# The modulation vector of a conditioned decoder: sixteen of its twenty-four pieces with the weights as the stationary operand

## The chip, the cores and the metric

The kernel runs on one core of a Trainium2 chip. The time is the device time of one execution in microseconds (us), the median over several runs. Engines are named as in the profile: PE (TensorE, matmuls; PEld are its loads of the stationary operand), DVE (VectorE), ACT (ScalarE), POOL (GpSimd), SP (SyncE, which here only issues transfers).

## The reference

One decoder layer works on 2048 prompt positions and 8 x 8 sample positions of width 1024. Shift, scale and gate of its two halves come from a conditioning vector: one row for the prompt, eight for the samples.

```python
def decoder_layer(x, c, ...):
    mod = jnp.einsum("bd,de->be", jax.nn.silu(c), w_ada) + b_ada      # w_ada: 1024 x 6144
    sh1, sc1, g1, sh2, sc2, g2 = jnp.split(mod[:, None, :], 6, axis=-1)
    h = x * (1.0 + sc1) + sh1
    mix, ... = mixer_block(h, ...)          # input projection, three token mixers, output projection
    x = layer_norm(DEEPNORM_ALPHA * x + g1 * mix, ln1_g, ln1_b)
    h2 = x * (1.0 + sc2) + sh2
    f = jnp.einsum("btf,fd->btd", jnp.square(jax.nn.relu(jnp.einsum("btd,df->btf", h2, w_up))), w_down)
    x = layer_norm(DEEPNORM_ALPHA * x + g2 * f, ln2_g, ln2_b)
```

## The kernel before

The prompt is worked in four groups of 512 positions, the samples ride with the last. First comes the mixer of each group: four slabs of w_in give the rows v (`v_slab`), twelve more (`fm_product`, F0 to F11) the other columns of the projection by features, DVE turns them into the mixer's three parts, and eight slabs of w_out close it. Then the MLP of all groups follows. Products are taken in three passes of a high and a low part (`mm3`); ACT and POOL make these parts from the raw slab, which SP fetches.

The modulation vector `mod` (9 rows x 6144) is computed in 24 pieces of 256 columns, `ada_product(u)` on PE. Each needs 1 MB of w_ada and the bias columns on 9 partitions. The 9 columns of silu(c), turned to features (`siluT`), are the stationary operand, the weights stream. The sums come out as 9 rows in PSUM; DVE adds the bias rows (`ada_add`, L1479), SP stores the rows to `mod_rows` in DRAM, from where the gates are later fetched. Shift and scale are needed by features, so PE turns every piece back with two transposes (`ada_turn`, L1110), and DVE copies the result into `modT` (`ada_turned`, L1488 and L1490; one is added to the scale). The semaphore `ada_T` counts these copies, and product u waits for the copy of piece u-2, whose bank it takes.

Pieces 0 to 7 are shift and scale of the first half, computed while the first group's x is turned (`x0_transposes`, L1159) and the first v slabs are worked. Pieces 8 to 23 stand in the stages of the first group's mixer, in an order written out by hand (`mixer_stages`): two after each of F0 to F3, one after each of F4 to F11. There `ada_turn(u-1)` follows `ada_product(u)` on PE, and `ada_add(u)`, `ada_turned(u-1)` stand behind the evacuation of the slab product on DVE. The stage "B" makes a bias table (DVE L1628), the stages "S" are the position mixing (DVE L1609). After piece 23 comes `second_modulation`, and then the next group's x is turned (`x_transposes`, L1219).

Of the kernel before, what the change touches and what calls it, by code (L numbers as in the profile page):

```python
# [233 lines left out]
def mixer_stages(s, vector):  # L234


    nt, first = tiles_of(s), s == 0
    F = [("F", n) for n in range(N_FM)]
    S01, S23 = ("S", [0, 1], 0 if nt == 4 else 1), ("S", [2, 3], 2 if nt == 4 else 3)
    if nt == 5:  # L240
        S4 = ("S", [4], 0)
        a = [S4, ("V", 1), F[0], ("V", 1)] if vector else [F[0], S4]
        a += [F[1], S01, ("V", 2), F[2], S23, F[3], F[4]]
    elif vector or first:
        a = [F[0], F[1], S01, ("V", 2), F[2], S23, F[3], F[4]]
    else:
        a = F[0:4] + [S01, F[4], S23]
    a += [F[5], F[6], F[7], ("M", 0), F[8], F[9], ("M", 1), F[10], F[11]]
    if first:
        out, u = [], ADA_FIRST  # L250
        for x in a:
            out.append(x)
            if x[0] == "F":
                for _ in range(2 if x[1] < 4 else 1):
                    out.append(("A", u))
                    u += 1
                if x[1] == 0:
                    out.append(("B", 0))
        a = out + [("E", u - 1)]
    return [x for x in a if vector or x[0] != "V"]  # L260


def decoder_layer_kernel(nc, x_prompt, x_sample, c_prompt, c_sample, state_conv, state_pool,
# [5 lines left out]
    with ctx:  # L269
# [66 lines left out]
        st = sb("st", [P, 5, 2, 6])  # L336
        siluT = sb("siluT", [P, KD * (1 + NB)])
        ln_now = (sb("mv", [P, 5, 2]), sb("rstd", [P, 5]), sb("rtmp", [P, 5]))
        ln_end = (sb("mv_end", [P, 5, 2]), sb("rstd_end", [P, 5]), sb("rtmp_end", [P, 5]))
# [43 lines left out]
        ada_mm = sem("ada_mm")  # L383
        ada_row = sem("ada_row")
        ada_tr = sem("ada_tr")
        ada_T = sem("ada_T")
        ada_out = [sem(f"ada_out{i}") for i in range(4)]
        x0_tr = sem("x0_tr")
# [108 lines left out]

        def ada_bias(u):
            return gs[0:1 + NB, ADA_COLS * (u % 4):ADA_COLS * (u % 4) + ADA_COLS]

# [16 lines left out]
        def _(sp):  # L517
# [5 lines left out]

            def ada_bias_in(u):
                if u >= 4:
                    sp.wait_ge(ada_tr, u - 3)
                    sp.wait_ge(ada_out[u % 4], 16 * (u // 4))
                sp.dma_start(ada_bias(u), bcast(b_ada[0, ada_col(u):ada_col(u) + ADA_COLS], 1 + NB)
                             ).then_inc(ada_in[u % 4], 16)

            def ada_rows_out(u):
                sp.wait_ge(ada_row, u + 1)
                sp.dma_start(mod_rows[:, ada_col(u):ada_col(u) + ADA_COLS], ada_bias(u)
                             ).then_inc(ada_out[u % 4], 16)
# [31 lines left out]
            for u in range(1, 3):  # L566
                ada_weights(u)
                ada_bias_in(u)
            x0_load(0)
# [54 lines left out]
            def weight_mix(g):  # L624
# [8 lines left out]
                for c, (after, buf) in enumerate(MIX_JOBS):  # L633
                    turn = [x for _, x in MIX_JOBS[0:c]].count(buf)
                    b, q, cols = mix_view(c)
                    if g == after:
                        if turn:
                            sp.wait_ge(mix_stored[buf], 16 * turn)
                        elif buf == 0:
                            sp.wait_ge(xs_tr, 1)  # L640
                        else:
                            sp.wait_ge(ada_tr, N_ADA)
                        for i in range(2):
# [45 lines left out]
            ada_weights(3)  # L689
            ada_bias_in(3)  # L690
            for n in range(2):
                slab(n, free=False)
            ada_rows_out(0)
            ada_piece(4)
# [21 lines left out]
            slab(21)  # L716
            for i in range(4):
                sp.wait_ge(ada_out[i], 16 * (N_ADA // 4))
            sp.dma_start(g1row[:, :], bcast(mod_rows[0, G1 * D:G1 * D + D], P)).then_inc(g1_loaded, 16)
# [368 lines left out]
        def _(pe):  # L1088
# [5 lines left out]
            def ada_product(u):  # L1094
                pe.wait_ge(ada_in[u % 4], 32 * (u // 4 + 1))
                if u >= 2:
# [3 lines left out]
                buf = ada_buffer(u)  # L1100
                for k in range(KD):
                    ins = pe.matmul(ps[0:1 + NB, 1 + 2 * (u % 2), 0:ADA_COLS],
                                    siluT[:, (1 + NB) * k:(1 + NB) * (k + 1)], buf[:, k, :],
                                    start=(k == 0), stop=(k == KD - 1))
                ins.then_inc(ada_mm, 1)

            def ada_turn(u):
                pe.wait_ge(ada_row, u + 1)
                for q in range(2):
                    ins = pe.transpose(ps[:, 1 + 2 * (u % 2), (1 + NB) * q:(1 + NB) * (q + 1)],  # L1110
                                       ada_bias(u)[:, P * q:P * q + P], ident[0:1 + NB, 0:1 + NB])
                ins.then_inc(ada_tr, 1)

            pe.wait_ge(s_c, 32)
            pe.wait_ge(s_ident, 1)
            for k in range(KD):
                ins = pe.transpose(ps[:, 0, (1 + NB) * k:(1 + NB) * (k + 1)],
                                   c_rows[0:1 + NB, P * k:P * k + P], ident[0:1 + NB, 0:1 + NB])
            ins.then_inc(s_cT, 1)
            pe.wait_ge(s_silu, 1)  # L1120
# [34 lines left out]
            def x0_transposes(k):  # L1155
                if k >= 2:
                    pe.wait_ge(x_tmp, k - 1)
                for t in range(4):
# [4 lines left out]
            def ada_next(u):  # L1163
                ada_product(u)
                ada_turn(u - 1)

            ada_next(1)
            for n in range(3):
                ada_next(2 * n + 2)
# [4 lines left out]
                ada_next(2 * n + 3)  # L1174
                if n < 2:
                    v_slab(0, n)
            ada_turn(ADA_FIRST - 1)
            x0_transposes(6)
# [44 lines left out]
            def mixer(s):  # L1223
# [5 lines left out]
                for stage in mixer_stages(s, False):  # L1229
# [35 lines left out]
                    elif stage[0] == "A":  # L1265
                        ada_product(stage[1])
                        if stage[1] > ADA_FIRST:
                            ada_turn(stage[1] - 1)
                    elif stage[0] == "E":
                        ada_turn(stage[1])  # L1270
                    else:
# [187 lines left out]
        def _(dve):  # L1459
# [22 lines left out]
            def ada_turned(u):  # L1482
                dve.wait_ge(ada_tr, u + 1)
# [3 lines left out]
                if q // KD == SC1:  # L1487
                    dve.tensor_scalar(dst, src, 1.0, None, ALU.add).then_inc(ada_T, 1)  # L1488
                else:
                    dve.tensor_copy(dst, src).then_inc(ada_T, 1)  # L1490

            def second_modulation():
                dve.wait_ge(ada_T, N_ADA)
                sh2, sc2 = (modT[:, q * KD:q * KD + KD, :] for q in (SH2, SC2))
                lng, lnb = (lnT[:, i, :].unsqueeze(2).to_broadcast([P, KD, 1 + NB]) for i in range(2))
                do(dve.tensor_scalar(sc2, sc2, 1.0, None, ALU.add))
                do(dve.tensor_tensor(scale2[:, :, :], sc2, lng, ALU.mult))
# [271 lines left out]
            def mixer(s):  # L1769
# [28 lines left out]
                for stage in mixer_stages(s, True):  # L1798
# [16 lines left out]
                    elif stage[0] == "A":  # L1815
                        ada_add(stage[1])
                        if stage[1] > ADA_FIRST:
                            ada_turned(stage[1] - 1)
                    elif stage[0] == "E":
                        ada_turned(stage[1])  # L1820
                        second_modulation()
# [26 lines left out]

            def ada_next(u):
                ada_add(u)  # L1850
                ada_turned(u - 1)

            ada_next(1)
            for n in range(3):
                ada_next(2 * n + 2)
                x0_feature(2 * n)
                x0_feature(2 * n + 1)
                ada_next(2 * n + 3)
            ada_turned(ADA_FIRST - 1)
            x0_feature(6)  # L1860
# [241 lines left out]
```

## Time and profile before

| | |
|---|---|
| median of 3 runs | 2225.09 us (2224.11 to 2225.3) |
| profiled execution | 2226.75 us, of it span 2225.0 us |
| PE busy | 2117.9 us, 95% |
| DVE busy | 1494.7 us, 67% |
| mean granted PE clock | 0.977 |

The profile is of one execution. Busy times of PE contain the latency of each pass, so that passes overlap in it: the distance between starts is the cost of one. A count of passes is twice that of plain fp32 matmuls, since each is run in two.

### The profile page before, as it was taken

To read this page: it belongs to the slowest core of one execution; us is meant where nothing else is said; L and a number is where in the kernel's file an instruction comes from. 1 tells how busy PE (TensorE), PEld (TensorE's weight loads), DVE (VectorE), ACT (ScalarE), POOL (GpSimd) and SP (SyncE) were. 2 spreads that over 40 slices of the span, in tenths; PEclk is the share of its full clock that TensorE was granted. 3 is DMA by queue.
4 is the path that set the end of the run, shared out by engine and by line. 5 is a ranking of instruction groups with operands and counts; after the bars stand their busy time and mean duration, and the time that the engine had idled before them with its cause. 6 is when DMAs were issued, how large, how long until landed. Compare 5 with 4: busy or idle time off the path is not lost.

```text
span 2225.0 us, 27801 instructions
## 1 busy us (share of the span) xinstructions
PE 2117.9 (95%) x10342; PEld 1750.2 (79%) x10342; DVE 1494.7 (67%) x2055; ACT 861.6 (39%) x1173; POOL 1448.8 (65%) x1109
## 2 busy tenths in 40 slices
PE   7989999999989999999989999989999999999995
PEld 4556787887889788888868888868888888999983
DVE  1554479678587665567778757687757777665677
ACT  1201322323212354445544545634454544444440
POOL 3323578685424367787777778867878866666664
PEclk9999999999999999999989999999999999999997
DMA  8546588695333254454624564534564533454331
GB/s 262 157 154 228 194 240 252 202 280 167 91 124 114 88 185 145 159 182 138 194 86 144 179 217 148 173 104 142 180 218 142 170 119 114 147 170 143 114 124 43
DMA packets 324089, 357.78 MB, mean 161 GB/s; under 512 B 16280, under 2 KB 256105, under 8 KB 323954
## 3 DMA queue, kind: packets, MB, share of 16 engines
q1 hardware_dynamic: 323954, 355.99, 50.7%
q8 instruction: 83, 1.36, 0.3%
q14 instruction: 52, 0.43, 0.1%
HBM read 321.34 MB, written 34.59 MB: 160 GB/s over the span
## 4 chain that ended last, share of the span: by engine, by line
PE 63%; DVE 11%; POOL 2%; issue 1%; ACT 1%; DVEq 0%; ACTq 0%
PE ps L1090 21%; PE ps L1092 20%; PE ps L1091 20%; PE ps L1354 1%; POOL acc L883 1%; DVE xt L1915 1%; DVE hid_a L1873 1%; POOL w_hilo L856 1%; DVE mix L1534 0%; DVE htmp L1716 0%; DVE pair_sums L1891 0%; PE ps L1423 0%; DVE acc L1977 0%; DVE pair_sums L1892 0%; DVE acc L1609 0%
## 5 line engine op out<-in xcount | busy, mean ns | idle before, releaser
L856 POOL TENSOR_TENSOR w_hilo<-w_raw,w_hilo 128x512 fp32r<-128x512 f32 x890 | 1270.1, 1456 | 719.5 <-ACT w_hilo L935 719.1
L935 ACT ACTIVATE w_hilo<-w_raw 128x1024 fp32r<-128x1024 f32 x445 | 469.9, 1058 | 720.3 <-PE ps L1092 610.3
L1090 PE MATMUL ps<-hA,w_hilo 128*128 128x512 f32 (+1 forms) x1760 | 621.9, 353 | 8.2 <-ACT htmp L993 3.2
L1091 PE MATMUL ps<-hA,w_hilo 128*128 128x512 f32 (+1 forms) x1760 | 620.3, 352 | 0.0
L1092 PE MATMUL ps<-hA,w_hilo 128*128 128x512 f32 (+1 forms) x1760 | 620.2, 352 | 0.0
L1090 PEld LDWEIGHTS ps<-hA,w_hilo 128*128 128x128 f32 x1760 | 332.2, 189 | 51.4 <-issue 7.5
L1091 PEld LDWEIGHTS ps<-hA,w_hilo 128*128 128x128 f32 x1760 | 332.3, 189 | 41.8
L1092 PEld LDWEIGHTS ps<-hA,w_hilo 128*128 128x128 f32 x1760 | 332.0, 189 | 41.5
L1965 DVE TENSOR_TENSOR acc<-acc,ps 128x512 f32<-128x512 f32 x270 | 178.4, 686 | 78.1 <-PE ps L1092 75.1
L1090 PE MATMUL ps<-w_hilo,hid_a 128*128 128x512 f32 x450 | 179.9, 400 | 25.8 <-DVE acc L1962 20.5
L1090 PE MATMUL ps<-w_hilo,hid_b 128*128 128x512 f32 x450 | 176.5, 392 | 1.6 <-POOL w_hilo L856 1.6
L1091 PE MATMUL ps<-w_hilo,hid_a 128*128 128x512 f32 x450 | 177.0, 393 | 0.0
L1092 PE MATMUL ps<-w_hilo,hid_a 128*128 128x512 f32 x450 | 176.8, 393 | 0.0
L1092 PE MATMUL ps<-w_hilo,hid_b 128*128 128x512 f32 x450 | 176.2, 392 | 0.0
L1091 PE MATMUL ps<-w_hilo,hid_b 128*128 128x512 f32 x450 | 176.1, 391 | 0.0
L986 ACT ACTIVATE htmp<-ps 128x512 f32<-128x512 f32 x96 | 57.2, 596 | 280.1 <-PE ps L1092 274.4
L1891 DVE TENSOR_TENSOR pair_sums<-htmp 128x256 f32<-128x256 f32 x62 | 33.2, 536 | 190.1 <-ACT htmp L996 189.8
L1090 PEld LDWEIGHTS ps<-w_hilo,hid_a 128*128 128x128 f32 x450 | 85.4, 190 | 44.4 <-issue 24.2
L1090 PE MATMUL ps<-w_hilo,mix 128*128 128x512 f32 (+1 forms) x272 | 109.4, 402 | 7.5 <-DVE mix L1534 7.5
L1091 PE MATMUL ps<-w_hilo,mix 128*128 128x512 f32 (+1 forms) x272 | 107.9, 397 | 0.0
L1092 PE MATMUL ps<-w_hilo,mix 128*128 128x512 f32 (+1 forms) x272 | 107.8, 396 | 0.0
L1090 PEld LDWEIGHTS ps<-w_hilo,hid_b 128*128 128x128 f32 x450 | 85.1, 189 | 20.3 <-POOL w_hilo L856 2.3
(233 smaller groups left out, 3000.2 us busy)
## 6 DMA issues: line engine op xcount, KB each, us to landing
w_raw<-in_w_up SPq DMA_DIRECT2D x128, 512.0 KB, 4.0
w_raw<-w_mix SPq DMA_DIRECT2D x124, 512.0 KB, 3.2
w_raw<-in_w_down SPq DMA_DIRECT2D x97, 512.0 KB, 3.6
w_raw<-in_w_in SPq DMA_DIRECT2D x64, 512.0 KB, 4.8
xt<-in_w_ada SPq DMA_DIRECT2D x22, 1024.0 KB
w_raw<-in_w_out SPq DMA_DIRECT2D x32, 512.0 KB, 4.8
xt<-x_norm SPq DMA_DIRECT2D x19, 512.0 KB, 5.7
xt<-in_w_down SPq DMA_DIRECT2D x36, 256.0 KB, 5.2
```

The source lines that it names most:

```text
L856: ins = pool.tensor_tensor(W[:, g % SLOTS, 1, cols], raw[:, g % RAW, cols], W[:, g % SLOTS, 0, cols], ALU.subtract)
L883: ins = pool.tensor_tensor(a, a, rows[:, G2_ROW, cols], ALU.mult)
L935: act.activation(W[:, g % SLOTS, 0, :], raw[:, g % RAW, :], ACT.Copy).then_inc(hi_done, 1)
L986: act.activation(x[:, 0:GT], ps[:, f % 2, :], ACT.Relu).then_inc(up_read, 1)
L1090: pe.matmul(out, w_hi, x_hi, start=start, stop=False)
L1091: pe.matmul(out, w_hi, x_lo, start=False, stop=False)
L1092: return pe.matmul(out, w_lo, x_hi, start=False, stop=stop)
L1354: pe.matmul(ps[:, 2 + h, :], x, W[:, w, part, HALF * p:HALF * p + HALF], start=start and part == 0, stop=False)
L1873: signal(dve.tensor_tensor(flat_part(h, 1, a, k), x, flat_part(h, 0, a, k), ALU.subtract), hid_ready, n)
L1891: do(dve.tensor_tensor(s1, a21, a22, ALU.add))
L1915: do(dve.scalar_tensor_tensor(x, x, ALPHA, acc[0:r, t, :], ALU.mult, ALU.add))
L1965: dve.tensor_tensor(a, a, src, ALU.add).then_inc(d_evac, 1)
```

## The change

The order of the columns over the pieces changes for u of 8 and more: even pieces are now gates (first G1, then G2), odd ones shift and scale of the second half. Gates keep the old way up to the rows, and have no transposes. The other sixteen pieces take each 128 x 128 block of weights as the stationary operand and stream the 9 columns of `siluT`: 16 matmuls of 9 columns, whose sums are already by features. Their bias is loaded once, as 48 rows of 128, turned by PE, and kept in `biasT` with one added at the scales; DVE adds it on the way to `modT`. Bias loads and row stores remain for the gates only.

```diff
-    return ADA_COLS * u
+    n = (u - ADA_FIRST) // 2
+    return ((G1, G2) if is_gate(u) else (SH2, SC2))[n // 4] * D + ADA_COLS * (n % 4)
+def is_gate(u):
+    return u >= ADA_FIRST and u % 2 == 0
...
             def ada_rows_out(u):
-                sp.wait_ge(ada_row, u + 1)
+                if is_gate(u):
+                    sp.wait_ge(ada_T, u + 1)
...
+            sp.dma_start(gs[0:6 * KD, 0:P], b_ada[0].rearrange("(q p) -> q p", p=P)).then_inc(s_c, 16)
             ada_weights(0)
-            ada_bias_in(0)
...
             for u in range(1, 3):
                 ada_weights(u)
-                ada_bias_in(u)
...
             def ada_product(u):
-                pe.wait_ge(ada_in[u % 4], 32 * (u // 4 + 1))
+                pe.wait_ge(ada_in[u % 4], 16 * (u // 4 + 1))
...
-                for k in range(KD):
-                    ins = pe.matmul(ps[0:1 + NB, 1 + 2 * (u % 2), 0:ADA_COLS],
-                                    siluT[:, (1 + NB) * k:(1 + NB) * (k + 1)], buf[:, k, :],
-                                    start=(k == 0), stop=(k == KD - 1))
+                bank = 1 + 2 * (u % 2)
+                if is_gate(u):
+                    for k in range(KD):
+                        ins = pe.matmul(ps[0:1 + NB, bank, 0:ADA_COLS], siluT[:, (1 + NB) * k:(1 + NB) * (k + 1)],
+                                        buf[:, k, :], start=(k == 0), stop=(k == KD - 1))
+                else:
+                    for q in range(2):
+                        for k in range(KD):
+                            ins = pe.matmul(ps[:, bank, (1 + NB) * q:(1 + NB) * (q + 1)], buf[:, k, P * q:P * q + P],
+                                            siluT[:, (1 + NB) * k:(1 + NB) * (k + 1)],
+                                            start=(k == 0), stop=(k == KD - 1))
                 ins.then_inc(ada_mm, 1)
...
-            def ada_turn(u):
-                pe.wait_ge(ada_row, u + 1)
-                for q in range(2):
-                    ins = pe.transpose(ps[:, 1 + 2 * (u % 2), (1 + NB) * q:(1 + NB) * (q + 1)],
-                                       ada_bias(u)[:, P * q:P * q + P], ident[0:1 + NB, 0:1 + NB])
-                ins.then_inc(ada_tr, 1)
...
-            def ada_add(u):
+            def ada_turned(u):
                 dve.wait_ge(ada_mm, u + 1)
-                dve.tensor_tensor(ada_bias(u), ps[0:1 + NB, 1 + 2 * (u % 2), 0:ADA_COLS], ada_bias(u),
-                                  ALU.add).then_inc(ada_row, 1)
...
+                if is_gate(u):
+                    dve.wait_ge(ada_rows_in[u // 2 % 2], 16 * (gate_turn(u) // 2 + 1))
+                    rows_ = ada_rows(u)
+                    dve.tensor_tensor(rows_, ps[0:1 + NB, 1 + 2 * (u % 2), 0:ADA_COLS], rows_,
+                                      ALU.add).then_inc(ada_T, 1)
+                    return
...
-                    dve.tensor_copy(dst, src).then_inc(ada_T, 1)
+                dve.tensor_tensor(dst, src, biasT[:, q:q + 2].unsqueeze(2).to_broadcast([P, 2, 1 + NB]),
+                                  ALU.add).then_inc(ada_T, 1)
...
                     elif stage[0] == "A":
-                        ada_add(stage[1])
-                        if stage[1] > ADA_FIRST:
-                            ada_turned(stage[1] - 1)
+                        ada_turned(stage[1])
```

PE around pieces 14 and 15, which follow F3 (the pool part). Before, from the end of F3 to the start of F4:

```order
L1092 MATMUL ps<-hA,w_hilo 128x512
L1102 MATMUL ps<-xt,siluT 9x256 [waits ada_T,ada_in2]
L1102 MATMUL ps<-xt,siluT 9x256 x7
L1110 MATMUL ps<-ident,gs 128x9 [waits ada_row]
L1110 MATMUL ps<-ident,gs 128x9
L1102 MATMUL ps<-xt,siluT 9x256 [waits ada_T,ada_in3]
L1102 MATMUL ps<-xt,siluT 9x256 x7
L1110 MATMUL ps<-ident,gs 128x9 [waits ada_row]
L1110 MATMUL ps<-ident,gs 128x9
L1090 MATMUL ps<-hA,w_hilo 128x512 [waits lo_done,fm_evac]
```

After, the same place (L1100 to L1102 are now the three passes of `mm3`, L1114 a gate piece, L1120 a feature piece):

```order
L1102 MATMUL ps<-hA,w_hilo 128x512
L1114 MATMUL ps<-xt,siluT 9x256 [waits ada_T,ada_in2]
L1114 MATMUL ps<-xt,siluT 9x256 x7
L1120 MATMUL ps<-siluT,xt 128x9 [waits ada_T,ada_in3]
L1120 MATMUL ps<-siluT,xt 128x9 x15
L1100 MATMUL ps<-hA,w_hilo 128x512 [waits lo_done,fm_evac]
```

Both pairs of transposes have gone; piece 15 has 16 matmuls in place of 8.

DVE at the same place. Before, from the end of the pool part's work (F3) to that of the u part (F4):

```order
L1534 TENSOR_TENSOR spl<-htmp,spl 128x512 [waits s_chain]
L1479 TENSOR_TENSOR gs<-ps,gs 9x256 [waits ada_mm,d_ready]
L1490 COPY modT<-ps 128x18 [waits ada_tr]
L1479 TENSOR_TENSOR gs<-ps,gs 9x256 [waits ada_mm]
L1490 COPY modT<-ps 128x18 [waits ada_tr]
L1745 TENSOR_TENSOR acc<-ps,acc 128x512 [waits slab_used]
```

After:

```order
L1546 TENSOR_TENSOR spl<-htmp,spl 128x512 [waits s_chain]
L1496 TENSOR_TENSOR gs<-ps,gs 9x256 [waits ada_rows_in1,ada_mm,d_ready]
L1502 TENSOR_TENSOR modT<-ps,biasT 128x18 [waits ada_mm]
L1757 TENSOR_TENSOR acc<-ps,acc 128x512 [waits slab_used]
```

The first L1490 before belongs to piece 13, the second to piece 14; L1496 after belongs to piece 14 and L1502 to piece 15. Piece 13's copy, on which PE's product 15 waits, now stands ahead of this place, behind F2.

## Rows read from the trace of the kernel before

**Rows 1.** The page, its first part: busy time, share of span, instructions.

```profile
PE 2117.9 (95%) x10342; PEld 1750.2 (79%) x10342; DVE 1494.7 (67%) x2055; ACT 861.6 (39%) x1173; POOL 1448.8 (65%) x1109
```

**Rows 2.** Stretches: length, busy by engine (PE, PEld, DVE, ACT, POOL), clock, DMA.

```profile
0.00:32.00 32.00, 17.76 (x80) 8.73 (x80) 4.25 (x10) 3.07 (x4) 6.04 (x45) 0.94 0.86 250
32.00:84.80 52.80, 52.28 (x244) 33.71 (x244) 20.41 (x48) 12.36 (x14) 29.98 (x24) 0.97 0.70 220
84.80:236.00 151.20, 137.23 (x621) 84.47 (x621) 75.75 (x150) 15.35 (x16) 46.08 (x36) 0.95 0.51 166
236.00:2225.00 1989.00, 1910.68 (x9400) 1623.33 (x9398) 1394.33 (x1850) 830.83 (x1139) 1366.67 (x1004) 0.98 0.50 157
```

**Rows 3.** Groups by form, 0 to 236 us: busy, mean ns, idle before.

```profile
L1102 PE MATMUL ps<-xt,siluT 128*9 128x256 f32 x352 | 85.9, 401 | 15.8 <-DVE modT L1490 9.7 <-DMA gs<-in_b_ada 6.1
...
L1479 DVE TENSOR_TENSOR gs<-ps,gs 9x256 f32<-9x256 f32 x24 | 9.9, 412 | 70.2 <-PE ps L1102 70.1
...
L1110 PE MATMUL ps<-ident,gs 9*128 9x9 f32 x48 | 6.9, 213 | 0.7 <-DVE gs L1479 0.7
```

**Rows 4.** PE's timeline, 14 to 236 us: start, duration, instructions, idle before.

```profile
14.63 1.04 PE L1130 MATMUL ps<-ident,g1row 128*128 128x128 f32 x8
17.26 3.62 PE L1102 MATMUL ps<-xt,siluT 128*9 128x256 f32 x16 [1.59 <-DMA gs<-in_b_ada]
...
37.47 0.50 PE L1090 MATMUL ps<-w_hilo,hA 128*128 128x512 f32 x1
...
43.13 3.62 PE L1102 MATMUL ps<-xt,siluT 128*9 128x256 f32 x16
46.69 0.29 PE L1110 MATMUL ps<-ident,gs 9*128 9x9 f32 x2
46.90 0.33 PE L1159 MATMUL ps<-ident,acc 128*128 128x128 f32 x1
...
109.22 5.30 PE L1102 MATMUL ps<-xt,siluT 128*9 128x256 f32 x16 [2.05 <-DVE modT L1490]
...
152.12 4.90 PE L1102 MATMUL ps<-xt,siluT 128*9 128x256 f32 x16 [6.47 <-DVE modT L1490]
...
235.81 1.06 PE L1219 MATMUL ps<-ident,xs 128*128 128x128 f32 x8 [0.36 <-DVE modT L1490]
```

**Rows 5.** PE's waits in the whole span: total us, times, longest.

```profile
PE ps L1102 <- DVE modT L1490: 9.7, 4, 6.5
...
PE ps L1110 <- DVE gs L1479: 0.7, 2, 0.4
```

**Rows 6.** DVE's timeline, 142 to 152 us.

```profile
142.02 0.17 DVE L1695 COPY acc<-pcarry 128x15 f32<-128x15 f32 x1 [1.63 <-PE ps L1092]
...
151.82 0.15 DVE L1490 COPY modT<-ps 128x18 f32<-128x18 f32 x1
```

**Rows 7.** PEld's timeline: loads of transposes, then full-width loads for 128 columns.

```profile
46.68 0.20 PEld L1110 LDWEIGHTS ps<-ident,gs 9*128 9x128 f32 x2 [0.43 <-issue]
...
617.89 0.18 PEld L1090 LDWEIGHTS ps<-wsS,spl 64*128 64x128 f32 x1 [0.16 <-issue]
...
619.12 0.19 PEld L1092 LDWEIGHTS ps<-wsS,spl 64*128 64x128 f32 x1
```

**Rows 8.** Stretches of 2 us; columns as in rows 2.

```profile
92.00:94.00 2.00, 1.01 (x8) 0.79 (x7) 1.26 (x4) 0.00 (x0) 0.21 (x1) 1.00 0.99 304
94.00:96.00 2.00, 0.94 (x6) 0.77 (x6) 0.84 (x2) 0.00 (x0) 0.00 (x0) 1.00 1.04 331
96.00:98.00 2.00, 1.94 (x6) 1.56 (x7) 1.39 (x3) 0.00 (x0) 0.00 (x0) 0.69 0.90 306
98.00:100.00 2.00, 2.00 (x7) 1.51 (x6) 0.00 (x0) 0.00 (x0) 0.00 (x0) 0.50 0.06 21
```

**Rows 9.** SP's timeline: the dearest small bias load, and the eight copies.

```profile
12.54 1.69 SPq L528 DMA_DIRECT2D gs<-in_b_ada  x1
...
17.63 6.00 SPq L578 DMA_DIRECT2D acc<-acc  x8
```

More of the change, by code:

```diff
@@ L259, in mixer_stages @@
         a = out + [("E", u - 1)]
-    return [x for x in a if vector or x[0] != "V"]
+    return [x for x in a if vector or x[0] not in ("V", "E")]
 def decoder_layer_kernel(nc, x_prompt, x_sample, c_prompt, c_sample, state_conv, state_pool,
@@ L383, in decoder_layer_kernel @@
         ada_mm = sem("ada_mm")
-        ada_row = sem("ada_row")
-        ada_tr = sem("ada_tr")
         ada_T = sem("ada_T")
-        ada_out = [sem(f"ada_out{i}") for i in range(4)]
+        ada_rows_in = [sem(f"ada_rows_in{i}") for i in range(2)]
+        ada_out = [sem(f"ada_out{i}") for i in range(2)]
+        s_biasT = sem("s_biasT")
         x0_tr = sem("x0_tr")
@@ L496, in ada_buffer, with ada_rows @@
             return t.rearrange("p t (a n) -> p (t a) n", a=4)
-        def ada_bias(u):
-            return gs[0:1 + NB, ADA_COLS * (u % 4):ADA_COLS * (u % 4) + ADA_COLS]
+        def ada_rows(u):
+            return gs[0:1 + NB, ADA_COLS * (2 + u // 2 % 2):ADA_COLS * (2 + u // 2 % 2) + ADA_COLS]
         def hid(b, pair):
@@ L522, in ada_weights, with ada_rows_load @@
                              ).then_inc(ada_in[u % 4], 16)
[L524 to L529, printed above, removed]
+            def ada_rows_load(u):
+                if is_gate(u):
+                    if gate_turn(u) >= 2:
+                        sp.wait_ge(ada_out[u // 2 % 2], 16 * (gate_turn(u) // 2))
+                    sp.dma_start(ada_rows(u), bcast(b_ada[0, ada_col(u):ada_col(u) + ADA_COLS], 1 + NB)
+                                 ).then_inc(ada_rows_in[u // 2 % 2], 16)
             def ada_rows_out(u):
-                sp.wait_ge(ada_row, u + 1)
-                sp.dma_start(mod_rows[:, ada_col(u):ada_col(u) + ADA_COLS], ada_bias(u)
-                             ).then_inc(ada_out[u % 4], 16)
+                if is_gate(u):
+                    sp.wait_ge(ada_T, u + 1)
+                    sp.dma_start(mod_rows[:, ada_col(u):ada_col(u) + ADA_COLS], ada_rows(u)
+                                 ).then_inc(ada_out[u // 2 % 2], 16)
             def ada_piece(u):
@@ L538, in ada_piece @@
                 ada_rows_out(u - 3)
-                ada_bias_in(u)
+                ada_rows_load(u)
             def x0_load(t):
@@ L567, in _ @@
                 ada_weights(u)
-                ada_bias_in(u)
             x0_load(0)
@@ L716, in _ @@
             slab(21)
-            for i in range(4):
-                sp.wait_ge(ada_out[i], 16 * (N_ADA // 4))
+            for i in range(2):
+                sp.wait_ge(ada_out[i], 16 * (N_ADA - ADA_FIRST) // 4)
             sp.dma_start(g1row[:, :], bcast(mod_rows[0, G1 * D:G1 * D + D], P)).then_inc(g1_loaded, 16)
@@ L1157, in x0_transposes @@
                     pe.wait_ge(x_tmp, k - 1)
+                elif k == 0:
+                    pe.wait_ge(s_biasT, 1)
                 for t in range(4):
@@ L1161, in x0_transposes @@
                 ins.then_inc(x0_tr, 1)
[L1163 to L1167, printed above, removed]
+            ada_product(1)
             for n in range(3):
-                ada_next(2 * n + 2)
+                ada_product(2 * n + 2)
                 if n == 0:
@@ L1475, in signal, with bias_turned @@
                 dve.wait_ge(sem_, value)
-            def ada_add(u):
-                dve.wait_ge(ada_mm, u + 1)
-                dve.tensor_tensor(ada_bias(u), ps[0:1 + NB, 1 + 2 * (u % 2), 0:ADA_COLS], ada_bias(u),
-                                  ALU.add).then_inc(ada_row, 1)
-            def ada_turned(u):
-                dve.wait_ge(ada_tr, u + 1)
+            def bias_turned():
+                dve.wait_ge(s_cT, 1)
+                do(dve.tensor_copy(biasT[:, :], ps[:, 4, 0:6 * KD]))
+                do(dve.tensor_scalar(biasT[:, SC1 * KD:SC1 * KD + KD], biasT[:, SC1 * KD:SC1 * KD + KD], 1.0, None,
+                                     ALU.add))
+                signal(dve.tensor_scalar(biasT[:, SC2 * KD:SC2 * KD + KD], biasT[:, SC2 * KD:SC2 * KD + KD], 1.0,
+                                         None, ALU.add), s_biasT, 1)
+            def ada_turned(u):
+                dve.wait_ge(ada_mm, u + 1)
+                if is_gate(u):
+                    dve.wait_ge(ada_rows_in[u // 2 % 2], 16 * (gate_turn(u) // 2 + 1))
[3 more added lines that the diff above has]
+                    return
                 q = ada_col(u) // P
@@ L1840, in mixer @@
                     signal(normalise(x, x, t, ln_end), xn_dve, 2 * s + t - 1)
-            ada_add(0)
+            bias_turned()
             dve.wait_ge(s_prepe, 1)
@@ L1847, in _ @@
             dve.tensor_copy(prep[:, 1, :].rearrange("p (b n) -> p b n", b=2), ps[:, 6:8, :]).then_inc(s_pret, 1)
[L1849 to L1853, printed above, removed]
+            ada_turned(0)
+            ada_turned(1)
             for n in range(3):
-                ada_next(2 * n + 2)
+                ada_turned(2 * n + 2)
                 x0_feature(2 * n)
                 x0_feature(2 * n + 1)
-                ada_next(2 * n + 3)
-            ada_turned(ADA_FIRST - 1)
+                ada_turned(2 * n + 3)
             x0_feature(6)
```

27 lines of the change are left out of this document (9 added, 18 removed).

## The prediction

> **What bounds the kernel now.** I read the table by stretches first, then the groups by line, PE's waits, and PE's and DVE's timelines inside the modulation part. PE is busy 95% of the span, the next engine 67% [rows 1]. The change touches only the first 236 us. In its first 32 us PE is busy for 17.8 us and the DMA engines for 0.86 of the time: transfers decide there. From 32 to 84.8 us PE is full (52.3 of 52.8), and from 84.8 to 236 it has 137 of 151 us [rows 2]. So from 32 us on, every PE nanosecond of the modulation pieces is on the path, and so is every PE wait; before that almost nothing of them is. After 236 us nothing is edited and PE stays full (1911 of 1989 us), so a gain or loss at 236 us is carried to the end.
>
> A piece now is 16 passes of a 256-column moving weight against 9 stationary columns (8 matmuls in fp32, two passes each), then two small transposes [rows 3]. A piece at the full clock takes 3.56 us to the start of the transposes, and the transposes 0.21 us to the next instruction: 43.13, 46.69, 46.90 [rows 4]. PE waits in this part are mostly one kind: the piece waits for DVE's copy of transposes, 9.7 us in four waits; two more, 0.7 us together, end at a transpose [rows 5]. The longest is 6.47 us, before 152.12. DVE's rows say why: the copy that releases it (151.82) stands behind the whole pooling step that began at 142.02 [rows 6]. After two of these waits, of 2.05 and 6.47 us, the piece takes 5.30 and 4.90 us in place of 3.62 [rows 4]: passes at about twice the distance at their start, as at 1.2 GHz in place of 2.4, after an idle engine. Elsewhere the table of clocks shows that level, 0.50 for 98 to 100 us [rows 8].
>
> **The change part by part.** Of 24 pieces, 8 (gates) keep their matmuls; 16 become 32 passes with 128 stationary and 9 moving columns.
>
> Removed transposes: 24 pairs. Two lie in the part that transfers decide, 22 behind it. 22 x 0.21 = 4.6 us gained.
>
> The new passes. No row shows a full-width fp32 weight with 9 moving columns. The nearest are the loads of 128 columns that are no transposes, 0.18 to 0.19 us each from start to end [rows 7]. What counts is the distance from one load to the next. Where 12 such full-width loads follow each other with short moving operands, the first starts at 617.89 and the last at 619.12: 1.23/11 = 0.112 us [rows 7]. 32 x 0.112 = 3.58 us a piece, against 3.56 now. With 0.1 us for the first load, which nothing covers, I take +0.1 us x 13 (the feature pieces from u = 3 on) = 1.3 us lost. Bounds: if the loads went like those of the small transposes, two in 0.20 us where a full-width transposing load lasts about 0.14, they would be some 0.064 us apart [rows 7], a piece 2.05 us, and the kernel gains 13 x 1.5 = 20 us more. If load and pass did not overlap at all, 0.188 each, a piece is 6.0 us and 13 x 2.5 = 32 us are lost. I take 0.112, since its row has the same kind of load (no transpose) and the same width. The Trainium skill (TensorE: Matmul & The Clock Gate, LDWEIGHTS) puts the load at its column count over 1.2 GHz whatever the rows, 107 ns for 128; by that alone a piece would be 3.4 us. It says too (Weight-path perf modes) that fp32 gets no faster weight load. The rule speaks against this change: moving 9 columns in place of 256 buys nothing, because the load takes the place of the stream, and the row above agrees.
>
> The waits. Now piece u waits for the copy of piece u-2, and DVE makes that copy in its turn of piece u-1, behind the evacuation of the slab product before it. After the change DVE empties piece u-2 in that piece's own turn, one turn earlier, which the order's rows show: no row of u-1 stands ahead of it. So in stages with two pieces the second no longer waits for the evacuation work between. All 9.7 us go, and the 0.7 us of the two at a transpose [rows 5]. What is late next at the long one: piece 14 (3.6), piece 15 (3.6) and slab product F4 (5.66, as 37.47 to 43.13) give PE 12.8 us after F3, while DVE is through with pooling and the two small copies 151.97 - 142.02 = 10 us after it begins, right behind F3 [rows 4, 6]. The next piece needs DVE only then: 3 us of room. In the second pooling step the room is wider. The transfers do not bite: a piece's 1 MB is issued when piece u-2 has ended, some 9 us or more before its use, and the DMA engines are half idle from 84.8 us on [rows 2].
>
> The clock after the waits: 5.30 + 4.90 - 2 x 3.62 = 3.0 us gained, since the idle time that went before is gone.
>
> At the end of the part PE still waits for DVE's last piece, about the 0.36 us it waits now; nothing gained.
>
> Off the path: DVE loses 24 additions of 0.41 us [rows 3], 16 of them replaced by copies that now add the bias, about 0.16 us as today's copies. It gains four small ones at the start, about 0.8 us, while PE waits for weights. SP loses 32 small DMAs of rows and biases. Three of them stand at the start, the dearest with 1.69 us of issue, and one comes in their place; but the x tiles that end the start are issued behind the 8 copies at 17.63, which wait for DVE's copy of the turned w_s and not for SP, so I put this at nothing [rows 9]. If SP did decide, it would be at most some 2 us of gain.
>
> Sum: 4.6 + 9.7 + 0.7 + 3.0 - 1.3 = 16.7 us. I take 16. The profiled execution has 2226.75 us (span 2225.0 and 1.75 around), 1.7 above the median of the runs; it would come to 2210.7, and the median of the runs, 2225.09, to 2209.
>
> **The rivals.**
> First: the clock. This is the one that ends on the other side. Between 92 and 96 us PE streams for half the time or less (busy 1.01 and 0.94 of 2 us, with latencies counted in), and the clock is down to 0.69 and 0.50 in the next two rows, 96 to 100 us [rows 8]. One such low stretch costs what the piece at 109.22 shows: 5.30 - 3.62 = 1.7 us [rows 4]. A pass of 256 columns takes 0.216 us ((3.62 - 0.38)/15, the last pass of a piece lasting 0.38), so 9 columns some 0.008 us of each 0.112. If the clock follows what streams through the array, a feature piece is emptier than that stretch was. If it follows whether PE has instructions in hand (loads or the drain of each pass included), a piece is full. Nothing before has loads without streaming, so the trace cannot tell. For the first view: 9-column stationary pieces hold the clock, so width does not matter, moving time may. For the second: even the 8 transposes at 14.63, followed by 1.6 us of waiting, left the piece at 17.26 at full clock, 3.62 us [rows 4]. The Trainium skill says of transposes that they do not count as busy (TensorE: Matmul & The Clock Gate, Part 4); this row speaks against it for these ones, and of weight loads the page says nothing. Price: 8 single pieces with one low stretch each, 8 x 1.7, and 5 in the stretch from 32 to 72 us where pieces stand close together and run at half speed themselves, 5 x 3.4: 30.6 us. Less the 16.7: +14, 2239 us. From half that price to 3.4 us for all 13 pieces, -1 to +27. It decides from about ten low stretches on.
>
> Second: the wait comes back elsewhere. If DVE is the bound of the slab stages, the 9.7 us and 3.0 us show up again as waits of slab products for evacuation. Then only 4 us are left: 2221. Against it: DVE is busy for half of the stretch from 84.8 to 236 us, 75.8 of 151.2 [rows 2].
>
> Third: loads do not overlap the passes (bound above): 16.7 - 32 = +15, 2240 us. The row with 0.112 speaks against it.
>
> Fourth: loads 0.064 us apart: 2209 - 20 = 2189.
>
> **How the numbers follow.** Forecast 0.46, clock 0.38, wait elsewhere 0.07, no overlap 0.04, cheap loads 0.05. The forecast's own range is 2203 to 2216 (load distance 0.105 to 0.12 is 13 x 32 x 0.007 = 3 us either way, waits 3 us). With the clock's case in, the range is 2203 to 2245; outside are the cheap loads and the worst of the clock, together under 0.2. What a measurement of this kernel can tell from no change is 0.2%, 4.5 us. Faster: 0.46, 0.05 and a part of the wait case and of the mild end of the clock: 0.56. Same 0.08, slower 0.36.
>
> **What would show it.** The groups of the pieces (now L1102) split into 8 gate pieces of 16 passes and 16 feature pieces of 32; the loads of the latter 188 ns long and 0.112 us apart; PE's wait on modT near 0.3 us in place of 9.7; the granted clock 1.00 from 36 to 236 us but for the stretch at 97 to 100; the first transposes of the next group of tiles at about 219 us in place of 235.81 [rows 4]. I am wrong if the windows behind feature pieces show 0.5 to 0.8 of the clock, if loads are 0.15 us or more apart, or if slab products wait for DVE where they did not.

## The result and the profile after

The changed kernel takes 2239.74 us (median of 4 runs, 2235.91 to 2240.24) beside 2225.2 us of the kernel before on the same chip: a ratio of 1.0053, 95% interval 1.0036 to 1.007. It is 14.5 us slower where 16 us of gain were forecast. The kernel before has medians of 2225.2 to 2230.5 us on the chips used below, so each run there is given as a ratio to it on the same chip too. The profiled execution has 2239.93 us and a span of 2238.2 us.

The stretches of the kernel after, with the bounds of [rows 2]; columns as there:

```profile
0.00:32.00 32.00, 25.32 (x121) 24.63 (x122) 2.81 (x9) 1.51 (x2) 6.04 (x45) 1.00 0.80 227
32.00:84.80 52.80, 51.89 (x249) 47.52 (x248) 9.84 (x21) 12.01 (x14) 20.17 (x17) 0.77 0.59 190
84.80:236.00 151.20, 148.72 (x736) 112.58 (x735) 79.93 (x149) 16.42 (x17) 52.88 (x42) 0.90 0.58 179
```

The column before the last two is the clock: 0.77 and 0.90 where [rows 2] have 0.97 and 0.95. PE looks busier than before (148.7 us against 137.2): its idle time went, and slow passes took its place. Even so the column says too little: up to the first fall that it shows, at 52 us here, it reads 1.00 whatever the passes do. Three passes of a slab product, each of 512 columns, start 1.28 us apart up to 46 us and 0.68 us apart behind it (next rows), so PE ran at half clock until about 46 us. Before, the first fall that it shows is at 28 us.

PE's timeline after: start, duration, instruction, idle before. L1114 is a gate piece, L1120 a feature piece, L1228 the turning of the next group's x:

```profile
17.63 7.00 PE L1120 MATMUL ps<-siluT,xt 128*128 128x9 f32 x32 [0.26 <-DMA xt<-in_w_ada]
24.48 6.98 PE L1120 MATMUL ps<-siluT,acc 128*128 128x9 f32 x32
...
34.16 7.00 PE L1120 MATMUL ps<-siluT,xt 128*128 128x9 f32 x32 [0.91 <-DMA xt<-in_w_ada]
41.01 0.77 PE L1100 MATMUL ps<-w_hilo,hA 128*128 128x512 f32 x1
42.44 0.63 PE L1100 MATMUL ps<-w_hilo,hA 128*128 128x512 f32 x1
43.72 0.63 PE L1100 MATMUL ps<-w_hilo,hA 128*128 128x512 f32 x1
...
47.51 0.39 PE L1100 MATMUL ps<-w_hilo,hA 128*128 128x512 f32 x1
48.19 0.39 PE L1100 MATMUL ps<-w_hilo,hA 128*128 128x512 f32 x1
...
48.87 3.63 PE L1120 MATMUL ps<-siluT,xt 128*128 128x9 f32 x32
52.36 0.31 PE L1173 MATMUL ps<-ident,acc 128*128 128x128 f32 x1
...
138.10 3.62 PE L1114 MATMUL ps<-xt,siluT 128*9 128x256 f32 x16
141.66 4.03 PE L1120 MATMUL ps<-siluT,xt 128*128 128x9 f32 x32
...
243.92 1.94 PE L1228 MATMUL ps<-ident,xs 128*128 128x128 f32 x8 [0.43 <-DVE modT L1502]
```

Three things stand here. A feature piece at full clock takes 3.63 us, passes (3.63 - 0.17)/31 = 0.112 us apart, the distance that [rows 7] gave (0.17 us is the length of the last pass). At half clock it takes 7.00 us, and the slab product behind it starts in the same state. And piece 15 at 141.66 follows its neighbour with no wait, where [rows 4] show 6.47 us before 152.12. The turning of x starts at 243.92 in place of 235.81, and its 8 transposes take 1.94 us in place of 1.06: the clock has fallen once more behind the last piece.

PE's waits after, whole span: none of a piece for DVE is left; [rows 5] had 9.7 us there.

```profile
PE ps L1120 <- DMA xt<-in_w_ada: 4.0, 3, 2.9
...
PE ps L1228 <- DVE modT L1502: 0.4, 1, 0.4
```

Stretches of 2 us after, around a pair of feature pieces (48.87 to 60.4, with the turning of eight tiles of x between them at 52.36):

```profile
50.00:52.00 2.00, 2.00 (x20) 2.00 (x20) 0.00 (x0) 0.00 (x0) 0.59 (x1) 1.00 0.03 8
52.00:54.00 2.00, 2.00 (x15) 2.00 (x15) 0.26 (x2) 0.81 (x2) 0.00 (x0) 0.70 0.06 18
54.00:56.00 2.00, 2.00 (x11) 2.00 (x11) 1.90 (x4) 1.69 (x2) 0.24 (x1) 0.50 0.95 333
...
64.00:66.00 2.00, 2.00 (x6) 1.61 (x5) 0.00 (x0) 0.00 (x0) 0.00 (x0) 0.50 0.00 0
66.00:68.00 2.00, 2.00 (x9) 1.58 (x9) 0.00 (x0) 0.00 (x0) 0.00 (x0) 0.89 0.00 0
```

PE is busy for the full 2 us in every row, and up to 56 us PEld too, and yet the clock falls to 0.50 and stays there into the slab product that begins at 60.4. No idle engine stands before this fall, unlike the ones of [rows 4].

**The balance.** What the clock takes can be read from such rows: (1 - clock) x length, with 0.5 for the time up to 46 us that the column misses. From 36 us to the turning of x it is 6.8 us before and 32.3 us after (27.3 by the column and 5.0). Piece 3 starts at 34.16 in place of 32.17, so the start costs 2.0 us. From there to the turning of x, before and after:

```profile
32.17:235.81 203.64, 189.31 (x862) 117.98 (x863) 95.87 (x195) 27.71 (x30) 76.06 (x60) 0.96 0.56 180
34.16:243.92 209.76, 206.85 (x1026) 166.00 (x1027) 90.99 (x174) 27.93 (x30) 75.71 (x60) 0.87 0.56 173
```

This stretch is 6.1 us longer. PE's idle time in it went from 14.3 to 2.9 us, 11.4 less, and 4.6 us of transposes went. Low clock in it is 33.2 us in place of 8.7, 24.5 more. Together that would be 8.5 us. Part of the rest is that a low stretch takes a little less than half of its length: passes of 512 columns are 0.427 us apart at half clock and 0.228 at full, 0.47 of it. That leaves some 0.9 us open. The turning of x moved by 2.0 + 6.1 = 8.1 us.

Behind the part the span grows by another 13.2 - 8.1 = 5.1 us. The code there is the same. The rows from there to 1080 us hold 17.1 us of low clock after and 11.9 before. Whether the change had a part in that is not shown: the run with 2 repeats below, as long in its first part, has 10.2 there.

### The profile page after: what moved, and what is told of

Its sections match the earlier page's. It is cut to its first block, busy times and chain, and to the rows that moved or that the text cites. A ratio compares the mean times of both kernels' runs of the same rounds, so it can differ in the third digit from the quotient of the medians.

```text
span 2238.2 us, 28147 instructions
## 1 busy us (share of the span) xinstructions
PE 2148.2 (96%) x10551; PEld 1818.4 (81%) x10551; DVE 1491.7 (67%) x2033; ACT 861.6 (38%) x1173; POOL 1449.6 (65%) x1109
## 4 chain that ended last, share of the span: by engine, by line
PE 63%; DVE 11%; POOL 2%; issue 1%; ACT 1%; DVEq 0%; ACTq 0%
PE ps L1100 20%; PE ps L1101 20%; PE ps L1102 20%; PE ps L1359 1%; POOL acc L893 1%; DVE xt L1920 1%; DVE hid_a L1878 1%; POOL w_hilo L866 1%; DVE htmp L1728 0%; DVE pair_sums L1896 0%; PE ps L1428 0%; DVE mix L1546 0%; DVE acc L1982 0%; DVE pair_sums L1897 0%; DVE acc L1621 0%
## 5 line engine op out<-in xcount | busy, mean ns | idle before, releaser
L1100 PE MATMUL ps<-hA,w_hilo 128*128 128x512 f32 (+1 forms) x1760 | 626.5, 356 | 8.1 <-ACT htmp L1003 3.2
L1102 PE MATMUL ps<-hA,w_hilo 128*128 128x512 f32 (+1 forms) x1760 | 623.8, 354 | 0.0
L1100 PEld LDWEIGHTS ps<-hA,w_hilo 128*128 128x128 f32 x1760 | 335.0, 190 | 54.1 <-issue 9.2
L1102 PEld LDWEIGHTS ps<-hA,w_hilo 128*128 128x128 f32 x1760 | 334.9, 190 | 42.5
L1100 PE MATMUL ps<-w_hilo,hid_a 128*128 128x512 f32 x450 | 179.7, 399 | 24.5 <-DVE acc L1967 20.5
L1100 PE MATMUL ps<-w_hilo,hid_b 128*128 128x512 f32 x450 | 176.6, 393 | 2.5 <-POOL w_hilo L866 2.5
L1102 PE MATMUL ps<-w_hilo,hid_a 128*128 128x512 f32 x450 | 176.6, 392 | 0.0
L1102 PE MATMUL ps<-w_hilo,hid_b 128*128 128x512 f32 x450 | 176.4, 392 | 0.0
L1100 PEld LDWEIGHTS ps<-w_hilo,hid_a 128*128 128x128 f32 x450 | 85.4, 190 | 43.2 <-issue 24.2
L1100 PE MATMUL ps<-w_hilo,mix 128*128 128x512 f32 (+1 forms) x272 | 109.4, 402 | 7.5 <-DVE mix L1546 7.5
L1102 PE MATMUL ps<-w_hilo,mix 128*128 128x512 f32 (+1 forms) x272 | 107.3, 394 | 0.0
L1100 PEld LDWEIGHTS ps<-w_hilo,hid_b 128*128 128x128 f32 x450 | 85.1, 189 | 21.0 <-POOL w_hilo L866 2.9
```

What stands on the lines that cost most here:

```text
L1100: pe.matmul(out, w_hi, x_hi, start=start, stop=False)
L1102: return pe.matmul(out, w_lo, x_hi, start=False, stop=stop)
```

## Experiments

Each run changes the changed kernel. The theories when the first four runs were chosen: A, the clock follows the time in which columns stream through the array, and weight loads do not count; B, the wide loads or the lack of transposes bring it down; C, the loss comes from the start or from the pieces' new order.

**14 repeats.** The same loads, but the 9 columns are streamed 14 times through a stride of zero; only the first nine sums are read.

```diff
-                            ins = pe.matmul(ps[:, bank, (1 + NB) * q:(1 + NB) * (q + 1)], buf[:, k, P * q:P * q + P],
-                                            siluT[:, (1 + NB) * k:(1 + NB) * (k + 1)],
-                                            start=(k == 0), stop=(k == KD - 1))
+                            r = repeats(u)
+                            out = ps[:, bank, PIECE * q:PIECE * q + (1 + NB) * r].rearrange("p (r n) -> p r n", r=r)
+                            x = siluT[:, (1 + NB) * k:(1 + NB) * (k + 1)].unsqueeze(1).to_broadcast([P, r, 1 + NB])
+                            ins = pe.matmul(out, buf[:, k, P * q:P * q + P], x, start=(k == 0), stop=(k == KD - 1))
```

(`repeats(u)` gives 14, PIECE is 128, and DVE reads its sums at 128 * q. The reading side is left out here.)

> The feature pieces stream each 9 columns of silu 14 times (126 columns in place of 9) against the same 32 weight loads; the extra sums are not read. Nothing else differs from the changed kernel. Theory A (the clock follows the time in which columns stream through the array): the granted clock stays at 1.00 from about 36 us to the end of the modulation part but for the stretch after the bias table, a pass still takes about 0.108 us because the load sets it, and the time falls to where the forecast had it without the clock's fall, 2208 to 2214 us. Theory B (the clock falls because of the wide loads themselves, or of the missing transposes, whatever streams): same clock as the changed kernel, 2240 us. Theory C (the loss is not the clock's but comes from the start or from the order of the pieces): 2235 to 2240 us.

Measured: 2209.48 us (2208.89 to 2210.38), ratio to the kernel before 0.9919 (0.9903 to 0.9934), within A's range. B and C fall: loads, order, and missing transposes are those of the changed kernel, and 30 us have gone. The pieces and the part's end:

```profile
7.39 5.55 PE L1130 MATMUL ps<-siluT,xt 128*128 128x126 f32 x32 [2.77 <-DMA xt<-in_w_ada]
17.41 3.84 PE L1130 MATMUL ps<-siluT,xt 128*128 128x126 f32 x32 [1.75 <-DMA xt<-in_w_ada]
...
212.30 3.73 PE L1130 MATMUL ps<-siluT,xt 128*128 128x126 f32 x32
216.46 1.07 PE L1236 MATMUL ps<-ident,xs 128*128 128x128 f32 x8 [0.43 <-DVE modT L1510]
```

A piece of 126-column passes lasts 3.73 us, (3.73 - 0.27)/31 = 0.112 us a pass: fourteen times the stream for no time. Already the second piece runs at full clock, though the clock falls once more in PE's wait for x (0.50 from 29 to 38 us).

**7, 4 and 2 repeats.** The same edit with r = 7, 4, 2.

> As the kernel with 14 repeats, with 7: 63 columns stream per load, some 0.05 us of each 0.108. Theory A: in between; the trace of before fell after a stretch that streamed for some 40% of its time, so at about half the clock may hold or fall now and then: 2210 to 2225 us. Theory B and C: 2240 us.

> As the kernel with 14 repeats, with 4: 36 columns stream per load, 0.03 us of each 0.108, less than the 40% after which the clock fell in the kernel before. Theory A: most feature pieces bring a fall again: 2226 to 2240 us. A theory by which only the almost empty passes of 9 columns count as idle (the drain of a pass counted in) would leave it near the kernel with 7 repeats, 2212 to 2218 us.

> With 2 repeats, 18 columns, 0.015 us of each 0.108. Theory A: as the changed kernel, 2234 to 2242 us.

Measured: 2215.5 (2212.32 to 2215.66; ratio 0.9942, 0.9925 to 0.9958), 2234.93 (2224.71 to 2241.16; ratio 1.0022, 1.0004 to 1.004) and 2239.48 us (2235.16 to 2241.26; ratio 1.0051, 1.0034 to 1.0068), each within the range that theory A gave it. The ten runs with 4 repeats scatter over 16 us. The table of stretches, from 36 to 84 and from 84 to 216 us, first with 14 repeats:

```profile
36.00:84.00 48.00, 48.00 (x297) 42.67 (x296) 18.43 (x41) 11.01 (x13) 29.75 (x24) 0.98 0.69 211
84.00:216.00 132.00, 128.48 (x715) 97.18 (x714) 72.02 (x129) 15.35 (x16) 45.54 (x36) 1.00 0.61 189
```

With 7 repeats, the same two stretches:

```profile
36.00:84.00 48.00, 48.00 (x290) 43.28 (x291) 15.12 (x27) 12.04 (x14) 27.89 (x22) 1.00 0.71 223
84.00:216.00 132.00, 128.47 (x693) 96.38 (x692) 74.19 (x141) 14.73 (x16) 45.77 (x36) 0.99 0.62 193
```

With 4 repeats:

```profile
36.00:84.00 48.00, 48.00 (x244) 43.71 (x245) 7.60 (x17) 9.40 (x11) 23.13 (x20) 0.82 0.59 183
84.00:216.00 132.00, 129.59 (x665) 98.82 (x663) 73.81 (x141) 15.36 (x16) 41.75 (x32) 0.92 0.60 186
```

With 2 repeats:

```profile
36.00:84.00 48.00, 48.00 (x233) 44.63 (x234) 6.78 (x17) 9.02 (x11) 18.93 (x16) 0.76 0.55 172
84.00:216.00 132.00, 129.59 (x650) 98.59 (x649) 72.15 (x140) 15.74 (x17) 44.64 (x34) 0.91 0.61 186
```

And the changed kernel, which streams the columns once:

```profile
36.00:84.00 48.00, 48.00 (x232) 44.21 (x232) 7.53 (x17) 9.80 (x12) 19.37 (x17) 0.75 0.55 174
84.00:216.00 132.00, 129.52 (x643) 98.10 (x643) 72.06 (x139) 14.75 (x16) 44.41 (x34) 0.90 0.59 181
```

PE's and PEld's busy columns hardly differ, the clock does. Here too the column reads 1.00 up to the first fall that it shows; by the distance of passes PE was at half clock until 45 to 48 us with 7, 4, 2 and 1 repeats. Of the 6.0 us by which the turning of x is later with 7 repeats than with 14 (222.47, 216.46), 4.6 lie at the start: the first four pieces all stay at the low clock, the fourth one 7.08 us long, and piece 8 begins at 88.64 in place of 84.09. The rest comes with a fall behind the bias table, from 99 to 103 us.

```profile
24.86 7.04 PE L1130 MATMUL ps<-siluT,acc 128*128 128x63 f32 x32
35.30 7.08 PE L1130 MATMUL ps<-siluT,xt 128*128 128x63 f32 x32 [1.21 <-DMA xt<-in_w_ada]
```

In this run the later pairs went on at a clock that was up (3.68 us a piece from 49 to 71 us), and the first four pieces, of the same passes, did not raise one that was down.

**14 repeats from piece 8 on.** r = 1 for pieces 0 to 7.

> 14 repeats for pieces 8 and later only, pieces 0 to 7 stream 9 columns as in the changed kernel. Theory A: the start and the stretch to piece 8 keep their loss (piece 8 begins at 99.8 us in the changed kernel and at about 85 to 88 in the kernel before), the mixer's stretch loses none: 2222 to 2229 us. Theory B and C: 2240 us.

Measured: 2227.06 us (2222.15 to 2228.21), ratio 0.9998 (0.9989 to 1.0008), as A had it. The clock is 0.73 from 36 to 84 us and 0.98 from 84 to 216. Of the 30 us between the changed kernel and 14 repeats, 17.6 belong to the pieces 0 to 7 and 12 to 13 to the rest.

**The wait put back.** With 14 repeats, from piece 9 on:

```diff
-                    pe.wait_ge(ada_T, u - 1)
+                    pe.wait_ge(ada_T, u if u > ADA_FIRST else u - 1)
```

> 14 repeats everywhere, and from piece 9 on a product waits for DVE's copy of the piece just before it, not of the one before that: about the wait that the kernel before had. If the waits of the kernel before cost what its rows show (9.7 us, and 3.0 us of low clock after them), this takes 9 to 14 us more than the kernel with 14 repeats and no such wait: 2219 to 2227 us. If they would have come back elsewhere (DVE bounds the stages), it takes less than 4 us more.

Measured: 2227.28 us (2222.73 to 2230.8), ratio 0.9994 (0.9983 to 1.0005): 17.8 us more than without the wait, above the range expected. The turning of x starts at 235.99 in place of 216.46. PE is busy for 135.1 us of 84.8 to 236 in place of 147.3, 12.1 us of waits, and the 2 us rows hold 8.9 us of low clock in place of 1.2: 19.8 together. (The profiled execution, 2230.8 us, is the slowest of the ten.) So this wait is not quite the old one: that had cost PE 10.4 us in all. Its largest part is:

```profile
PE ps L1130 <- DVE gs L1504: 9.4, 3, 6.6
```

**The transposes put back.** With 14 repeats, behind every piece:

```diff
+                for q in range(2):
+                    ins = pe.transpose(ps[:, bank, 384 + (1 + NB) * q:384 + (1 + NB) * (q + 1)],
+                                       ident[0:1 + NB, :], ident[0:1 + NB, 0:1 + NB])
```

> 14 repeats, and every piece, gates too, is followed by the two small transposes that were removed, here of the identity and into columns that nothing reads. If a pair costs the 0.21 us that its rows show, 22 pairs behind the start cost 4.6 us: 2213 to 2215 us. If they were hidden, 2209 to 2210 us.

Measured: 2217.94 us (2216.98 to 2220.03), ratio 0.9956 (0.994 to 0.9972), 8.5 us more than without them, nearly twice what was expected. Behind a gate piece a pair does cost 0.22 us (88.78 to 89.00):

```profile
88.78 0.29 PE L1132 MATMUL ps<-ident 9*128 9x9 f32 x2
89.00 3.17 PE L1130 MATMUL ps<-siluT,xt 128*128 128x126 f32 x26
```

Behind a feature piece it costs 0.39 us, for the next product starts 3.88 us after the piece with a pair and 3.49 without:

```profile
159.97 3.73 PE L1130 MATMUL ps<-siluT,xt 128*128 128x126 f32 x32
163.63 0.28 PE L1132 MATMUL ps<-ident 9*128 9x9 f32 x2
163.85 0.50 PE L1107 MATMUL ps<-hA,w_hilo 128*128 128x512 f32 x1
```

The same place without the pairs:

```profile
156.10 3.73 PE L1130 MATMUL ps<-siluT,xt 128*128 128x126 f32 x32
159.59 0.48 PE L1107 MATMUL ps<-hA,w_hilo 128*128 128x512 f32 x1
```

From piece 3 on there are 13 feature pieces and 8 gates, 13 x 0.39 + 8 x 0.22 = 6.8 us; piece 3 itself was 0.7 us shorter in this run, because the clock rose earlier. That is the 5.95 us by which the turning of x starts later (222.41 in place of 216.46). The other 2.1 us of the spans' difference, 8.1, are two of PE's waits for DVE behind the part: the wait for `mix` is 8.0 us in place of 7.0, the one before the turning of the next x 2.7 in place of 1.6. So the expectation had the price of a pair behind a gate piece right and that behind a feature piece wrong.

**Short streams without wide loads.** The feature pieces leave out their sums but for 2 of the 16 products; 25 matmuls with silu stationary and 9 columns of weights moving stand in their place.

```diff
-                        for k in range(KD):
-                            ins = pe.matmul(ps[:, bank, (1 + NB) * q:(1 + NB) * (q + 1)], buf[:, k, P * q:P * q + P],
...
+                        pe.matmul(ps[:, bank, (1 + NB) * q:(1 + NB) * (q + 1)], buf[:, 0, P * q:P * q + P],
+                                  siluT[:, 0:1 + NB], start=True, stop=True)
+                    for i in range(25):
+                        k = i % KD
+                        ins = pe.matmul(ps[0:1 + NB, bank, 256:256 + 1 + NB], siluT[:, (1 + NB) * k:(1 + NB) * (k + 1)],
+                                        buf[:, k, 0:1 + NB], start=True, stop=True)
```

> The feature pieces leave out their sums but for 2 of the 16 products; in their place stand 25 matmuls (50 passes) with the 9 columns of silu stationary and 9 columns of weights moving: short streams without wide loads. Passes should be about 0.064 us apart as the small transposes were, a piece 3.5 us at full clock. Theory A (streaming time counts, whatever the load): the clock falls behind these pieces as in the changed kernel, the whole 2235 to 2245 us. If wide loads were needed for the fall, the clock stays at 1.00: 2207 to 2213 us.

Measured: 2197.97 us (one run; its outputs are wrong, since sums are left out, as in the two runs behind it). It tells nothing on the question, because the passes were only 0.025 us apart and not 0.064:

```profile
47.66 1.41 PE L1123 MATMUL ps<-xt,siluT 128*9 128x9 f32 x50
```

(1.41 - 0.17)/49 = 0.025. The piece was 1.9 us long in place of 3.5. So the run was made again with 60 matmuls, and with 2 moving columns in place of 9:

> As the run with narrow loads, whose 50 passes took only 0.0256 us each, so that a piece lasted 1.9 us in place of 3.6 and the clock hardly had an emptier stretch than before. Here 60 matmuls (120 passes) of 9 columns against 9 stationary columns make the piece 3.5 us long at full clock; most of the sums are left out as before. 9 columns stream in 0.0075 us of 0.0256, 29%. Theory A (streaming time alone): as with 4 repeats, 28%: the clock falls behind most pieces and 10 to 20 us are lost to it up to the end of the modulation part. A theory by which wide loads are needed for the fall, or by which the number of passes counts: the clock stays at 1.00 but for the stretch behind the bias table.

> The same with 2 moving columns a pass: 0.0017 us of 0.0256, 7%, the share of the changed kernel's pieces. Theory A: the clock falls as in the changed kernel, 20 us or more lost to it in the part. If passes in flight count (each fills the array for a while, whatever it streams), the clock stays at 1.00.

Measured: 2220.99 and 2233.78 us (one run each). Low clock from 36 us to the turning of x, with the time that the column misses: 16.1 us with 9 columns, 32.5 us with 2. The same two stretches as above, with 9 columns:

```profile
36.00:84.00 48.00, 46.42 (x755) 41.15 (x755) 16.24 (x27) 12.48 (x14) 28.06 (x23) 1.00 0.72 227
84.00:216.00 132.00, 129.20 (x1305) 97.74 (x1304) 69.92 (x137) 13.55 (x15) 42.27 (x34) 0.91 0.61 192
```

With 2 columns:

```profile
36.00:84.00 48.00, 46.18 (x717) 41.23 (x716) 9.85 (x21) 11.66 (x14) 23.38 (x20) 0.79 0.64 203
84.00:216.00 132.00, 129.59 (x1192) 98.38 (x1191) 71.99 (x138) 14.31 (x15) 40.22 (x31) 0.88 0.59 185
```

Both came out as theory A expected. With 2 columns the stream takes 7% of a pass, as in the changed kernel, and the low clock is the same, 32.5 and 32.3 us, with narrow loads and nearly four times as many passes: the fall does not need the wide load, and that many passes do not prevent it. With 9 columns, 29% of a pass, the low clock is 16.1 us where the 4 repeats (27%, wide loads, fewer passes) have 26.2, and the close pieces up to 84 us bring no fall. With one profile each, that difference stays open: the share of streaming need not be the whole of it. Streaming a column and writing its sums to PSUM also go together in all these runs, and none parts them.

The kernels with 1 to 14 repeats beside each other. "Streamed" is the share of a pass that its columns take, from 0.216 us for 256 columns and the measured distance of passes; "low clock" is the sum of (1 - clock) x length from 36 us to the turning of x, with 0.5 where the column misses it. It is of one execution, whose time is given; the ratio is of all:

| kernel | columns a pass | streamed | low clock, us | that execution, us | ratio to before |
|---|---|---|---|---|---|
| before | 256 (rows) | 1.00 | 6.8 | 2226.75 | 1 |
| after | 9 | 0.07 | 32.3 | 2239.93 | 1.0053 |
| 2 repeats | 18 | 0.14 | 33.1 | 2235.16 | 1.0051 |
| 4 repeats | 36 | 0.27 | 26.2 | 2236.68 | 1.0022 |
| 7 repeats | 63 | 0.47 | 6.2 | 2215.61 | 0.9942 |
| 14 repeats | 126 | 0.95 | 1.2 | 2208.89 | 0.9919 |

## Why the prediction was wrong

The step that failed is the choice between two readings of the clock. The forecast gave 0.46 to "the clock follows whether PE has instructions in hand" and put the fall behind feature pieces at nothing; it gave 0.38 to the rival "it follows what streams through the array". The runs bear out the rival: with the same loads in the same order the clock stays up with 126 columns a pass and falls with 9, and that is 30 us of the whole.

The rival's mechanism and its places were right, its number in part by luck. It had 30.6 us of loss less 16.7 of gains, +14, all of it up to the turning of x. There the changed kernel is 27.5 us behind the run with 14 repeats, and that run 19.35 ahead of the kernel before: +8.1. The 5.1 us that bring the spans' difference to 13.2 (+14.5 between the medians) came behind the part, where the rival had none.

- **Passes.** 0.112 us foretold, 0.112 measured, with 9 as with 126 columns. By the Trainium skill (TensorE: Matmul & The Clock Gate, LDWEIGHTS) it would be 0.107: the trace is 0.005 above it. The 0.1 us a piece on top, 1.3 us in all, did not come: at full clock the next instruction starts 3.49 to 3.60 us behind the start of a feature piece, 3.56 behind that of an old one.
- **Transposes.** 0.21 us a pair by [rows 4], 0.22 when put back behind a gate piece. The 4.6 us hold; that putting them back cost 8.5 is due to the 0.39 us of a pair behind a feature piece and to waits behind the part.
- **Waits.** In the run with 14 repeats PE's idle time from piece 3 to the turning of x is 4.0 us in place of 14.3: the 10.4 us foretold are gone, and none came back elsewhere. Put back, a slightly longer wait (12.1 us) cost 17.8.
- **Clock behind the waits.** Foretold 3.0 us of gain. In the run with 14 repeats the low clock of the part went from 6.8 to 1.2 us, 5.6: the fall behind the bias table at 97 us [rows 8] went too.
- **Start.** I put it at nothing. Piece 3 starts 2.0 us later, for the first pieces never leave the low clock: 6.97 us for the first of them in place of 5.58.
- **The sum without the fall.** 16 us of gain were forecast. The run with 14 repeats shows 18.0 (2209.48 beside 2227.51 on its chip, so that it meets the 2209 of the forecast is partly luck). In its part 19.35 us went (235.81 to 216.46), where the terms as measured, 10.4 + 5.6 + 4.6, give 20.6; a part of that is again that a low stretch costs less than half its length.

Where the reasoning went astray: the piece at 17.26 at full clock behind eight transposes was counted for "instructions in hand". Those transposes stream 128 columns each, so that row fitted both readings. The numbers of [rows 8] fitted both too, for PE stood idle for half of that stretch. So 0.46 against 0.38 was a guess, and the prediction said itself that the trace could not tell. The Trainium skill says that transposes do not count as busy (the same page, Part 4); that row speaks against it for these eight, and no run here tests it further.

## What to carry to other kernels

Choosing which operand stands still is also choosing the clock of what follows: a pass that loads 128 columns and streams 9 costs the same time as one that streams 126, but PE pays for it afterwards at half speed, and the busy columns of the profile do not show it. Read the granted clock behind such a stretch, and the distance of passes beside it, since the clock column can read 1.00 at half speed up to its first fall. Where the load sets the pace, stream the moving operand several times through a stride of zero: it costs nothing and here turned 14.5 us of loss into 18 us of gain. A wait of PE of a few microseconds costs its length and then the low clock behind it: here 12.1 us of waits brought 7.7 us of low clock.

## What the runs showed of the hardware

- The clock falls with PE busy throughout: 0.50 from 54 us on with both PE columns at 2.00 of 2.00. Back-to-back loads of 128 columns do not hold it (after), and 120 narrow passes a piece do not either (2 moving columns).
- With 7 repeats four pieces from 7.5 us on stayed at 1.2 GHz (7.04 to 7.09 us each), while the later pairs of the same passes stayed at 2.4 GHz (3.68 us each); with 14 repeats the clock rose within the first piece (5.55 us long).
- Loads of 128 columns with short streams are 0.112 us apart at full clock and 0.213 at half (of the piece at 17.63 in the changed kernel, the first 12 passes take 2.73 us and the first 30 take 6.57). Passes with 9 stationary and 9 moving columns in fp32 follow each other every 0.025 us, at either level: 120 take 3.16 us at 8.27 us, where the wide passes beside them are at half speed, and 3.15 us at 48.09.
- Up to the first fall that it shows, the clock column reads 1.00 also where passes run at half speed, up to 46 us in the changed kernel.
